# Attention of a decoder layer: the sample's score, key-turn and eviction entries of slots 0 to 4 of twelve, spread between scores, values and turns of the probabilities

## The chip, the cores and the metric

The kernel runs on one core of a Trainium2 chip. The metric is the device time of one execution in microseconds (us). PE is TensorE, ACT is ScalarE, DVE is VectorE, POOL is GpSimd, SP is SyncE, which issues most of the transfers.

## The reference

One layer of a decoder trunk: a half-step feed-forward block, a mixing block with three branches, a second feed-forward block. It serves a prompt of 1024 tokens and eight samples of eight new tokens with 2048 cached keys each. The attention stage of the kernel computes these parts:

```python
def sparse_core(q, k_sel, v_sel, valid):
    s = jnp.einsum("bthd,btkhd->bthk", q, k_sel, preferred_element_type=jnp.float32) * (DH_ATT ** -0.5)
    s = jnp.where(valid[:, :, None, :], s, -jnp.inf)
    p = jax.nn.softmax(s, axis=-1).astype(v_sel.dtype)
    o = jnp.einsum("bthk,btkhd->bthd", p, v_sel)
...
def mem_attend(qm, mk, mv):
    s = jnp.einsum("bthd,bmhd->bthm", qm, mk, preferred_element_type=jnp.float32) * (DH_MEM ** -0.5)
    p = jax.nn.softmax(s, axis=-1).astype(mv.dtype)
    o = jnp.einsum("bthm,bmhd->bthd", p, mv)
```

In `dsa_sample` the keys and values of a sample lie in 16 pages of 128 tokens, found through `page_table`; which keys count is decided before the attention stage and comes into it as a bias (`bias` for the prompt, `bias_s` for the samples).

## The kernel before

The attention stage works off 96 jobs of the prompt, one in each **slot**. A head h (0 to 7) has twelve slots: slots 0 to 7 are the blocks of 128 queries i = 0, 7, 1, 6, 2, 5, 3, 4 of the prompt's own attention, so that slots with few keys, (i + 1) * 128, and many keys alternate; slots 8 to 11 are blocks of the attention to 256 memory tokens. While head h of the prompt is worked off, sample b = h is done beside it, piece by piece. So "head 3" below stands for twelve slots: 12 * 3 + 0 to 12 * 3 + 11, and its sample is number 3.

`attention_plan` writes one list of entries, and every engine walks this list from the first to the last, doing its part of each entry in that order. In a slot s stand, before the change:

- `scores` of job s (PE: three matmuls for each 512 keys, into banks 0/1 or 2/3; DVE: the maximum, then a small product);
- `oturn`, in slot 2 of each head (and slot 10 of odd ones): PE turns finished outputs, 4 blocks at a time;
- `values` of job s - 2 (PE, into bank 6; DVE scales the result: "norm" below);
- `turn` of job s - 1: PE turns the probabilities, up to four blocks of 128 x 128 in one entry;
- `exp` of job s (ACT);
- the sample's entries of this slot, from the table `slots`: `("kt", u)` turns one page u of keys with four transposes, `("sc", g)` makes the sample's scores from four turned pages (PE: eight instructions in bank 5; ACT copies 512 columns out, line L2851).

Each of `turn`, `oturn`, `kt` and some others is a *turning entry*: it needs one of only two banks, `turn_bank = [bank[4], bank[7]]`, and takes them alternately. The entry with an even number is copied out by ACT, the one with an odd number by DVE, and PE may not start a turning entry before the copy of the last but one is finished:

```python
            if turn is not None and turn >= 2:

                wait_turn(pe, turn - 2)
```

Since the number of turning entries before slot 0 differs, the sides change from head to head: of slots 1 to 3 in odd heads (1, 3, 5, 7) page 4 goes to DVE before the change, in even heads to ACT.

The keys' pages come by DMA into `k_ring`, six pages deep. SP issues page n after page n - 6 has been turned, and one page of values (`v_ring`) after each page of keys, 256 KB each. `kt4` holds the turned keys of two groups of four pages, and `sc` of group g waits until its four pages have been copied there.

Of the kernel before, what the change touches and what calls it, by code (L numbers as in the profile page):

```python
# [2331 lines left out]
def attention_plan():  # L2332

    jobs = []
    for h in range(H):  # L2340
        jobs += [("att", i, h) for i in (0, 7, 1, 6, 2, 5, 3, 4)] + [("mem", h % 2 * 4 + i, h // 2) for i in range(4)]
    slots = [
# [6 lines left out]
        [("soft",), ("msc",)],  # L2349
        [("pt", 0), ("pt", 1), ("pt", 2), ("pt", 3), ("pt", 4)],  # L2350
        [("pv",), ("mpt",)],
        [("mpv",), ("ot",)],
        [("mot",)],
        [],
    ]
    plan = []
    turns = 0

    def add(*entry):
        nonlocal turns  # L2360
        turn = None
        if entry[0] in ("turn", "oturn", "kt", "pt", "mpt", "ot", "mot"):
            turn = turns
            turns += 1
        plan.append((entry, turn))

    n = len(jobs)
    add("stack", 0)
    for s in range(n + 3):
        if s < n:  # L2370
            add("scores", s)
        if 0 <= s - 3:

            kind, i, h = jobs[s - 3]
            if kind == "att" and i == 4 and h % 2 == 1:
                add("oturn", s - 3, 0)
                add("oturn", s - 3, 1)
            if kind == "mem" and i % 4 == 3:
                add("oturn", s - 3, 0)
        if 0 <= s - 2 < n:  # L2380
            add("values", s - 2)
        if s >= n - 2:

            add("merge", s - n + 2)
        if 0 <= s - 1 < n:
            kind, i, h = jobs[s - 1]
            blocks = i + 1 if kind == "att" else 2
            for g in range(0, blocks, 4):
                add("turn", s - 1, g, min(4, blocks - g))
        if s < n:  # L2390

            add("exp", s)
            for e in slots[s % 12]:
                add(e[0], s // 12, *e[1:])
            if s % 12 == 8 and s // 12 + 1 < H:
                add("stack", s // 12 + 1)
    return jobs, plan


def attention(nc, sem, mem, bank, bank_t, ident, ident16, qT, kT, qmT, mkT, mv, rq, bias, bias_s, rep, I, O, tail, heads):  # L2400

    jobs, plan = attention_plan()
    at = AT_X + 8192
    def place(name, shape, dt, size):
# [868 lines left out]
```

## Time and profile before

| what | value |
|---|---|
| median of three runs | 3210.53 us (3206.44 to 3211.04) |
| the profiled execution | 3222.86 us, span 3221.3 us |
| PE busy | 3096.3 us of the span, 96% |
| slots 0 to 4 of the eight heads together | 222.10 us, PE busy in 203.70 of them |
| attention stage | from 1684.7 us to about 2157 us of the span |

The page of the profile gives shares of the whole span; the other stages are 85% of it. The attention stage has to be read by itself, slot by slot. A slot begins with the first matmul of its scores (L2684 for the prompt's own attention), so its length is the distance to the first matmul of the next slot's scores.

### The profile page before, as it was taken

The page shows a single profiled execution, that of the slowest core. Times are in us where ns is not written, and L with a number is a line of the kernel's source. Part 1 is how long each engine was busy: PE and PEld are TensorE (multiplying, and loading weights), DVE is VectorE, ACT ScalarE, POOL GpSimd, SP SyncE. Part 2 cuts the span into 40 slices and gives each one's busy share as a digit, 9 for nine tenths or more (in the row PEclk, how much of TensorE's full clock was granted, in tenths as well). Part 3 has the DMA queues.
Part 4 walks back from the last instruction along what each step waited for, and adds up shares of the span by engine and source line. Part 5 has one row for each costly group of instructions (what it writes and reads, how often), then busy time and mean ns, then how long its engine had stood idle before and what let it go on. Part 6 is the DMA issues. An engine that isn't in the chain of part 4 may idle for free. (4 is left out here: it accounts for less than half of the span.)

```text
span 3221.3 us, 51712 instructions
## 1 busy us (share of the span) xinstructions
PE 3096.3 (96%) x19690; PEld 2914.6 (90%) x19690; DVE 1735.3 (54%) x3041; ACT 911.6 (28%) x1616; POOL 668.7 (21%) x415
## 2 busy tenths in 40 slices
PE   7999999999899999999799999889999999999999
PEld 7999999999899999998756666669999999999998
DVE  6333333333669999999535555555645333333333
ACT  5111111111433332334344444441231111111111
POOL 2211221222443321222250000012121212221120
PEclk9999999999999999999888999999999999999999
DMA  3111111111322222221445446344421111111111
GB/s 115 41 45 39 52 39 45 46 46 40 89 82 86 81 85 83 64 74 55 146 133 195 160 146 219 126 164 143 137 73 39 41 46 46 46 39 46 39 46 62
DMA packets 256495, 265.47 MB, mean 82 GB/s; under 512 B 14575, under 2 KB 197458, under 8 KB 256334
## 3 DMA queue, kind: packets, MB, share of 16 engines
q1 hardware_dynamic: 250858, 254.61, 25.0%
q0 software_dynamic: 4128, 4.20, 0.5%
q10 hardware_dynamic: 1348, 4.49, 0.4%
q8 instruction: 103, 1.69, 0.2%
q14 instruction: 58, 0.48, 0.0%
HBM read 226.20 MB, written 37.05 MB: 82 GB/s over the span
## 5 line engine op out<-in xcount | busy, mean ns | idle before, releaser
L331 PE MATMUL bank<-h_hi,w_hi 128*128 128x362 f32 (+1 forms) x3384 | 1119.0, 331 | 25.9 <-DVE sg_ffn L513 7.7
L331 PE MATMUL bank<-h_lo,w_hi 128*128 128x362 f32 (+1 forms) x3384 | 1113.2, 329 | 0.0
L331 PE MATMUL bank<-h_hi,w_lo 128*128 128x362 f32 (+1 forms) x3384 | 1111.9, 329 | 0.0
L331 PEld LDWEIGHTS bank<-h_hi,w_hi 128*128 128x128 f32 x3384 | 638.5, 189 | 33.3 <-issue 18.4
L331 PEld LDWEIGHTS bank<-h_lo,w_hi 128*128 128x128 f32 x3384 | 638.9, 189 | 2.9 <-issue 0.3
L331 PEld LDWEIGHTS bank<-h_hi,w_lo 128*128 128x128 f32 x3384 | 638.7, 189 | 0.0
L388 POOL TENSOR_TENSOR w_lo<-raw,w_hi 128x1024 fp32r<-128x1024 f32 x132 | 316.5, 2406 | 1272.9 <-ACT w_hi L483 1272.9
L550 DVE SCALAR_TENSOR_TENSOR x<-bank,x 128x362 f32<-128x362 f32 (+1 forms) x528 | 280.5, 535 | 213.6 <-PE bank L331 213.6
L331 PE MATMUL bank<-a_hi_ffn,w_hi 128*128 128x362 f32 (+1 forms) x1056 | 347.6, 329 | 5.5 <-DVE x L550 3.8
L331 PE MATMUL bank<-a_lo_ffn,w_hi 128*128 128x362 f32 (+1 forms) x1056 | 346.5, 328 | 0.0
L331 PE MATMUL bank<-a_hi_ffn,w_lo 128*128 128x362 f32 (+1 forms) x1056 | 346.2, 328 | 0.0
L513 DVE TENSOR_TENSOR sg_ffn<-bank,drs_ffn 128x364 f32<-128x364 f32 x132 | 70.4, 535 | 393.9 <-PE bank L331 393.7
L518 DVE TENSOR_TENSOR up_ffn<-bank,drs_ffn 128x364 f32<-128x364 f32 x132 | 70.7, 535 | 372.1 <-PE bank L331 372.1
L483 ACT CAST w_hi<-raw 128x1024 fp32r<-128x1024 f32 x132 | 136.1, 1046 | 426.5 <-PE bank L331 426.5
L1309 POOL TENSOR_TENSOR w_lo<-raw,w_hi 128x1024 fp32r<-128x1024 f32 x53 | 128.3, 2421 | 394.4 <-ACT w_hi L1533 394.4
L331 PEld LDWEIGHTS bank<-a_hi_ffn,w_hi 128*128 128x128 f32 x1056 | 198.4, 188 | 7.9 <-DVE x L550 5.7
L331 PEld LDWEIGHTS bank<-a_lo_ffn,w_hi 128*128 128x128 f32 x1056 | 198.5, 188 | 0.1
L331 PEld LDWEIGHTS bank<-a_hi_ffn,w_lo 128*128 128x128 f32 x1056 | 198.5, 188 | 0.0
L499 ACT CAST a_hi_ffn<-pr_ffn 128x364 fp32r<-128x364 f32 x132 | 65.7, 498 | 433.3 <-DVE pr_ffn L525 433.3
L3048 POOL TENSOR_TENSOR w_lo<-raw,w_hi 128x1024 fp32r<-128x1024 f32 x20 | 50.3, 2520 | 637.0 <-ACT w_hi L3097 637.0
L493 ACT ACTIVATE sg_ffn<-sg_ffn 128x364 f32<-128x364 f32 x132 | 66.9, 509 | 391.3 <-DVE sg_ffn L513 391.2
L1898 DVE MAX8 top<-S 128x8 f32<-128x384 f32 (+5 forms) x192 | 171.2, 891 | 4.1
(370 smaller groups left out, 4138.6 us busy)
## 6 DMA issues: line engine op xcount, KB each, us to landing
raw<-in_w_ffn_in SPq DMA_DIRECT2D x88, 512.0 KB, 3.8
k_ring<-in_cache_k SPq DMA_DIRECT2D x128, 256.0 KB, 4.0
v_ring<-in_cache_v SPq DMA_DIRECT2D x128, 256.0 KB, 4.3
raw<-in_w_in SPq DMA_DIRECT2D x53, 512.0 KB, 4.9
raw<-in_w_ffn_out SPq DMA_DIRECT2D x44, 512.0 KB, 3.4
kept_g<-stage SPq DMA_DIRECT2D x24, 544.0 KB, 3.1
gate<-kept_g SPq DMA_DIRECT2D x24, 544.0 KB, 3.6
x<-x_kept SPq DMA_DIRECT2D x8, 544.0 KB, 4.3
```

The lines of the kernel that those rows point to most:

```text
L331: mm = pe.matmul(out, left, right, start=(start and i == 0 and j == 0), stop=(stop and i == n - 1 and j == 2))
L388: pool.tensor_tensor(self.w_lo[:, u % 3, :], self.raw[:, u % 3, :], self.w_hi[:, u % 3, :].bitcast(F32), ALU.subtract).then_inc(self.low, 1)
L483: act.copy(self.w_hi[:, u % 3, :], self.raw[:, u % 3, :]).then_inc(self.high, 1)
L493: act.activation(self.sg[:, c, 0:w], self.sg[:, c, 0:w], ACT.Silu).then_inc(self.silu_done, 1)
L499: act.copy(self.a_hi[:, t, t0:t0 + w], self.pr[:, c, 0:w]).then_inc(self.prod_high, 1)
L513: dve.tensor_tensor(sg[:, c, 0:w], bank[c][:, 0:w], rs[:, t0:t0 + w], ALU.mult).then_inc(self.scaled, 1)
L518: dve.tensor_tensor(up[:, c % 2, 0:w], bank[3 + c][:, 0:w], rs[:, t0:t0 + w], ALU.mult).then_inc(self.up_scaled, 1)
L550: dve.scalar_tensor_tensor(self.x[:, j, t0:t0 + w], bank[:, 0:w], 0.5, self.x[:, j, t0:t0 + w], ALU.mult, ALU.add).then_inc(self.x_added, 1)
L1309: pool.tensor_tensor(w_lo[:, n % 3, :], raw[:, n % 3, :], w_hi[:, n % 3, :].bitcast(F32), ALU.subtract).then_inc(low, 1)
L1898: after(dve.max(top8[0:rows, :], scores))
L3048: pool.tensor_tensor(w_lo[:, n % 3, :], raw[:, n % 3, :], w_hi[:, n % 3, :].bitcast(F32), ALU.subtract).then_inc(low, 1)
```

## The change

The table of the sample's entries stays as it is, and so does the work. Slots 0 to 4 of each head ("early") place the entries of their slot at three places in place of one: the first entry straight after `scores`, the next two after `values`, and the rest where they all were, after `exp`. Slot 4 has only one entry, `sc 3`, which moves up whole.

```diff
     n = len(jobs)
+    def sample(s, a, b=None):
+
+        if s < n:
+            for e in slots[s % 12][a:b]:
+                add(e[0], s // 12, *e[1:])
+
     add("stack", 0)
     for s in range(n + 3):
+        early = s % 12 < 5
         if s < n:
             add("scores", s)
+            if early:
+                sample(s, 0, 1)
...
         if 0 <= s - 2 < n:
             add("values", s - 2)
+        if early:
+            sample(s, 1, 3)
...
             add("exp", s)
-            for e in slots[s % 12]:
-                add(e[0], s // 12, *e[1:])
+            sample(s, 3 if early else 0)
```

The first place is PE's queue in slots 1 and 2 of an even head (2). `k_high`/`q_stack` with `bias` are the prompt's scores, `bias_s` and `kt` the sample's scores, `mv` and `vp` the values, `pb` the turn of the probabilities, `o_m` the turn of outputs, `k_ring` the turn of pages, four transposes each. Before, from the last matmul of slot 1's scores to the first of slot 3's:

```order
L2686 MATMUL bank<-bias_66,ident_10_58 128x512
L2711 MATMUL bank<-mv_12474,pt_12526 128x128 x2
L2693 MATMUL bank<-ident_55,pb_12525 128x128
L2739 MATMUL bank<-bias_s_67,rep_68 32x512 x4
L2744 MATMUL bank<-kt_121_12518,qbd_12529 32x512 x4
L2724 MATMUL bank<-ident_55,k_ring_12524 128x128 x16
```

```order
L2686 MATMUL bank<-bias_66,ident_10_58 128x256
L2718 MATMUL bank<-ident_55,o_m_12532 128x128 x4
L2707 MATMUL bank<-vp_12520,pt_12526 128x64
L2693 MATMUL bank<-ident_55,pb_12525 128x128 x8
L2739 MATMUL bank<-bias_s_67,rep_68 32x512 x4
L2744 MATMUL bank<-kt_121_12518,qbd_12529 32x512 x4
L2724 MATMUL bank<-ident_55,k_ring_12524 128x128 x16
```

The same two stretches after the change (all line numbers there are higher by ten):

```order
L2696 MATMUL bank<-bias_66,ident_10_58 128x512
L2749 MATMUL bank<-bias_s_67,rep_68 32x512 x4
L2754 MATMUL bank<-kt_121_12518,qbd_12529 32x512 x4
L2721 MATMUL bank<-mv_12474,pt_12526 128x128 x2
L2734 MATMUL bank<-ident_55,k_ring_12524 128x128 x8
L2703 MATMUL bank<-ident_55,pb_12525 128x128
L2734 MATMUL bank<-ident_55,k_ring_12524 128x128 x8
```

```order
L2696 MATMUL bank<-bias_66,ident_10_58 128x256
L2749 MATMUL bank<-bias_s_67,rep_68 32x512 x4
L2754 MATMUL bank<-kt_121_12518,qbd_12529 32x512 x4
L2728 MATMUL bank<-ident_55,o_m_12532 128x128 x4
L2717 MATMUL bank<-vp_12520,pt_12526 128x64
L2734 MATMUL bank<-ident_55,k_ring_12524 128x128 x8
L2703 MATMUL bank<-ident_55,pb_12525 128x128 x8
L2734 MATMUL bank<-ident_55,k_ring_12524 128x128 x8
```

The sample's scores stood between the turns of the probabilities and the four pages; now they stand ahead of all turning entries of the slot, and the turns of the probabilities stand between the second and the third page.

The second place is ACT's queue from slot 1 to the exponentials of slot 2, in the same kind of head. `pt` is the copy of turned probabilities, `kt` of a turned page, `ps` of the sample's scores, `pb` the exponentials. Before:

```order
L2511 COPY pt_12526<-bank 128x128
L2841 ACTIVATE pb_12525,stats_12539<-bank,stats_12539,rq_12475 128x1024
L2851 COPY ps_12527<-bank 128x512
L2532 COPY kt_121_12518<-bank 128x4x128 x2
L2511 COPY pt_12526<-bank 128x512
L2841 ACTIVATE pb_12525,stats_12539<-bank,stats_12539,rq_12475 128x256
```

And after:

```order
L2861 COPY ps_12527<-bank 128x512
L2542 COPY kt_121_12518<-bank 128x4x128
L2521 COPY pt_12526<-bank 128x128
L2851 ACTIVATE pb_12525,stats_12539<-bank,stats_12539,rq_12475 128x1024
L2542 COPY kt_121_12518<-bank 128x4x128
L2861 COPY ps_12527<-bank 128x512
L2542 COPY kt_121_12518<-bank 128x4x128
L2521 COPY pt_12526<-bank 128x512
L2851 ACTIVATE pb_12525,stats_12539<-bank,stats_12539,rq_12475 128x256
```

The copy of the sample's scores and the first of ACT's two pages now stand ahead of the slot's exponentials; the second stays behind them.

## Rows read from the trace of the kernel before

**Rows 1.** The page: span, and PE's busy time, share and instructions.

```profile
span 3221.3 us, 51712 instructions
...
PE 3096.3 (96%) x19690; PEld 2914.6 (90%) x19690; DVE 1735.3 (54%) x3041; ACT 911.6 (28%) x1616; POOL 668.7 (21%) x415
```

**Rows 2.** Page turns in the attention stage: PE's idle time before them, times, by releaser.

```profile
  DVE kt L2532: 17.2, 39
  ACT kt L2532: 17.0, 31
  DMA k_ring<-in_cache_k: 4.7, 6
```

**Rows 3.** Busy time by window: slots 0 to 4 of heads 0 and 4; all eight.

```profile
1684.72:1717.19 32.47, 26.78 (x176) 17.53 (x174) 12.39 (x27) 13.49 (x26) 0.81 (x5) 0.84 0.93 310
...
1923.04:1950.15 27.11, 25.36 (x189) 17.22 (x188) 14.01 (x34) 12.92 (x27) 0.00 (x0) 0.96 0.78 258
...
sum 222.10, PE 203.70 PEld 136.16 DVE 112.41 ACT 103.52 POOL 0.81; mean PE 25.46 PEld 17.02 DVE 14.05 ACT 12.94 POOL 0.10
```

**Rows 4.** Windows, slots 0 to 4 of head 3: length, PE, PEld, DVE, ACT, POOL, clock, DMA.

```profile
1863.66:1867.79 4.13, 3.65 (x28) 2.76 (x27) 2.34 (x7) 2.52 (x7) 0.00 (x0) 1.00 0.01 2
1867.79:1873.65 5.86, 5.51 (x42) 3.30 (x41) 3.47 (x7) 2.55 (x6) 0.00 (x0) 1.00 0.82 291
1873.65:1879.78 6.13, 5.71 (x49) 3.77 (x47) 3.34 (x8) 3.14 (x7) 0.00 (x0) 1.00 0.92 296
1879.78:1886.74 6.96, 6.61 (x56) 4.69 (x54) 3.15 (x7) 2.85 (x6) 0.00 (x0) 1.00 0.93 321
1886.74:1889.92 3.18, 3.18 (x29) 1.79 (x27) 2.21 (x6) 1.73 (x4) 0.00 (x0) 1.00 0.94 317
```

**Rows 5.** Windows, slots 0 to 2 of head 4.

```profile
1923.04:1927.71 4.67, 4.48 (x28) 3.66 (x26) 2.60 (x8) 1.82 (x6) 0.00 (x0) 0.76 0.00 0
1927.71:1933.99 6.28, 5.38 (x42) 3.30 (x41) 3.10 (x7) 3.00 (x6) 0.00 (x0) 1.00 0.88 289
1933.99:1940.00 6.01, 5.60 (x48) 3.79 (x47) 2.98 (x8) 3.34 (x7) 0.00 (x0) 1.00 0.94 316
```

**Rows 6.** The timeline of slots 0 and 1 of head 3.

```profile
1865.26 1.93 PE L2724 MATMUL bank<-ident,k_ring 128*128 128x128 f32 x12
...
1866.76 0.34 SPq L2611 DMA_DIRECT2D k_ring<-in_cache_k  x1
...
1867.23 0.59 ACT L2532 COPY kt<-bank 128x512 f32<-128x512 f32 x1 [0.75 <-PE bank L2724]
...
1867.38 0.66 PE L2724 MATMUL bank<-ident,k_ring 128*128 128x128 f32 x4 [0.19 <-DVE kt L2532]
...
1867.79 0.48 PE L2684 MATMUL bank<-k_high,q_stack 128*128 128x512 f32 x1
...
1868.07 0.69 DVE L2532 COPY kt<-bank 128x512 f32<-128x512 f32 x1 [0.75 <-PE bank L2724]
...
1869.92 0.40 PE L2739 MATMUL bank<-bias_s,rep 64*32 64x512 bf16 x4
...
1870.93 1.21 ACT L2841 ACTIVATE pb<-bank,stats,rq 128x1024 f32<-128x1024 f32 x1 [0.64 <-DVE stats L2897]
...
1871.24 1.09 PE L2724 MATMUL bank<-ident,k_ring 128*128 128x128 f32 x8
...
1872.68 1.22 PE L2724 MATMUL bank<-ident,k_ring 128*128 128x128 f32 x8 [0.35 <-DVE kt L2532]
```

**Rows 7.** Windows of head 0: end of slot 2, slot 3; slot 10, slots 11 to 0.

```profile
1696.60:1702.33 5.73, 2.41 (x20) 1.30 (x13) 1.48 (x3) 1.79 (x5) 0.00 (x0) 1.00 0.96 317
1702.72:1714.01 11.29, 11.29 (x56) 7.75 (x54) 2.73 (x6) 3.22 (x6) 0.00 (x0) 0.55 0.95 334
...
1741.20:1744.40 3.20, 1.75 (x13) 1.14 (x12) 2.83 (x10) 1.03 (x3) 0.00 (x0) 1.00 0.24 87
1744.40:1751.20 6.80, 6.79 (x31) 5.92 (x31) 3.42 (x15) 2.72 (x8) 0.00 (x0) 0.50 0.00 0
```

## The prediction

> **What bounds the kernel now.** I read the page first: PE is busy 96% of a span of 3221.3 us [rows 1], so a change of order can only win where PE waits. Then the windows of the attention stage: slots 0 to 4, the only ones that the change touches, take 222.10 us over the eight heads, and PE is busy in 203.70 of them, so 18.4 us are idle [rows 3]. Head 0 alone has 32.47 - 26.78 = 5.7 of these; the other seven have 12.7, or 1.8 each. Slot by slot, head 3 idles 0.48, 0.35, 0.42 and 0.35 us in slots 0 to 3 and nothing in slot 4 [rows 4]. Head 4 idles 0.9 in slot 1 [rows 5]. Last I asked who ends these waits at the page turns: copies of turned pages by DVE and ACT, 34.2 of 38.9 us (PE's own and the weight loads' idle time added up); pages that had not landed, 4.7 [rows 2]. Neither ACT (12.92 of 27.11) nor DVE (14.01) is full [rows 3]. The bound is PE, with the return of the two turning banks behind it.
>
> **The price of a bank.** All steps below rest on four durations of [rows 6]. Four transposes are issued in 0.41 us (1867.38 to 1867.79), in 0.50 where another group follows at once (my reading of pairs, an estimate between 0.41 and half of 1.09). A copy starts 0.69 after its group (1867.38 to 1868.07) and takes 0.69 on DVE, 0.59 on ACT. So a bank is free again 1.44 us after its group began where DVE copies: the page groups at 1871.24 and 1872.68 show just that. Where ACT copies it is 1.34. The sample's scores cost PE 1.32 (1869.92 to 1871.24) and need no turning bank: they are the cover behind which banks come back.
>
> Before the change, slot 1 is scores, values and a one-block turn (2.13), the sample's scores (1.32), and four pages (1872.68 - 1871.24 = 1.44 for the first pair with its wait, 0.97 for the second): 5.86, as [rows 4] has it. A slot pays one bank wait among its four pages, and the turns of the probabilities pay almost none, since the sample's scores and the prompt's scores stand on either side of them.
>
> **The change part by part.** No instruction is added or taken away; SP's and POOL's queues keep their order. What moves is the place of pages and sample's scores among the others on PE, ACT and DVE, so waits alone change.
>
> *Slots 1 and 3.* The row of turning entries is now page, page, turn, page, page without a gap. The third page needs the bank of the second, or of the turn, whichever is later; the second began 0.50 after the first, so the stretch from the first page to the next slot is 0.50 + 1.44 + 0.85 (the last pair) = 2.79 where DVE has the even places, 2.69 where ACT has. Slot 1: 2.13 less the turn's 0.20, plus 1.32, plus 2.79 = 6.04 in an odd head (before 5.86), 5.94 in an even one (before 6.28 [rows 5]). The even head gains 0.34: there ACT's exponentials of 1.21 us and its copy of the sample's scores stood ahead of the first page's copy, and now stand behind it. Slot 3, the same row behind longer scores and values: +0.2 odd, +0.1 even.
>
> *Slot 2.* The row is seven entries long: turned outputs, page, page, turn, turn, page, page; only values of one block stand in it. The first, third, fifth and seventh share a bank, so the seventh starts three returns after the first: 3 x 1.44 + 0.41 = 4.73 in odd heads, 3 x 1.34 + 0.35 = 4.37 in even ones. Ahead of it, the sample's scores now come straight behind the prompt's, and these are short here (256 keys, about 0.48, an estimate from the 1.9 of slot 1's scores and values). They need the last page of slot 1 copied, 1.34 to 1.44 after it began, of which its own issue and the scores cover 0.83: a new wait of 0.51 to 0.61 on PE, with everything of the slot queued behind it. Slot 2: 0.48 + 0.51 + 1.32 + 4.73 = 7.04 (before 6.13), even 0.48 + 0.61 + 1.32 + 4.37 = 6.78 (before 6.01). This is the largest term, +0.9 and +0.8.
>
> *Slot 4.* The same wait in front of its only entry, behind scores of 384 keys: +0.4 odd, +0.5 even, in a slot of 3.18 that had no idle time [rows 4].
>
> *Slot 0.* Page 0 now starts some 0.3 after the slot began, where PE waited for the turned probabilities of the slot before, and covers that wait. Three pages and the turn follow. Odd heads: 3.65 for 4.13, -0.5. In even heads the clock is low at first (0.76 in the mean [rows 5]); the transposes take twice as long and I find 4.60 for 4.67.
>
> *Pages.* Page 6 is asked for 1.5 us after page 0's turn begins (1865.26, 1866.76 [rows 6]), and the stream runs on at 291 to 321 GB/s with the DMA engines 0.82 to 0.93 busy [rows 4]. Page 0 is turned some 1.3 us earlier, and page 15 later, so the waits for pages (4.7 us in all [rows 2]) should go, except head 0's, whose stream starts when the stage before lets it.
>
> **Sum.** Odd head 3.65 + 6.04 + 7.04 + 7.16 + 3.57 = 27.5, against 26.25 in head 3 [rows 4]. Even head 4.60 + 5.94 + 6.78 + 7.05 + 3.67 = 28.0, against 27.11 in head 4 [rows 3]. Four odd and three even heads make 194.0, plus 1.2 for head 1's slot 0, which runs in the low clock that follows 1744.40 [rows 7]: 195.2 against 222.10 - 32.47 = 189.6. That is +5.6; head 0 is held by its pages up to slot 2 and gets +0.3 in slot 4: **+5.9 us**. The profiled execution (3222.86 us, 1.6 beyond its span) would come to 3228.8; the median of the runs stands 12.3 lower, so 3210.53 + 5.9 = 3216.4. Bounds of the unknown parts: the new waits of slots 2 and 4 lie between 0 (if copies finish under the scores) and 0.6 each, 0 to 9 us over all; slot 2's row between its issue time (3.3) and 4.73. I take the upper ends, since [rows 6] shows the return of 1.44 with no slack, and let the lower ones widen the range.
>
> **Rivals.**
> (a) *Slower still, by the clock.* In head 0 PE is busy in 2.41 of 5.73 us before slot 3, and the clock then falls: slot 3 takes 11.29 for head 3's 6.96. Slot 10 idles 1.45 of 3.20, and 6.80 us at 0.50 follow [rows 7]; heads 2, 4 and 6 idle as long there and keep the clock, so it is near a border. The change shifts those stretches and thins slot 2 (3.3 of issue in 4.7). One fall costs about 1.8 us (head 1's slot 0 alone shows 1.2); three more make 3222. Against it: slot 2 stays two thirds busy. The Trainium skill, "TensorE: Matmul & The Clock Gate", section "A second HAM failure mode: psum-queue depth-cycling", says that PE idling briefly between groups while it cycles through banks lets the clock fall again and again. By that rule every slot 2 would be slow; the trace does not bear it out for four pages in a row, which run at 1.00 [rows 4].
> (b) *Faster, by the pages.* If the page stream set the length of slots 1 to 3, an earlier page 0 would pull all in: 1.3 us in seven heads, 9 us, 3201. For it: 0.93 of the DMA engines. The Trainium skill, "DMA: Bandwidth & Descriptors", section "Specifications", gives about 358 GB/s as the limit of HBM for a core, which the 321 is near. Against it: pages end only 4.7 of 38.9 us. It decides only if PE reaches page 15 before it lands, and my slots 2 and 3 move PE the other way.
> (c) *Faster, as cover.* Spreading hides the bank waits altogether: the seven heads' 12.7 us go, 3198. It needs the turn of the probabilities to find a free bank behind two pages; with two banks and a return of 1.34 it can't.
> (d) *No change.* The waits only change places, and shorter ones than I find in slots 2 and 4 balance slots 0 and 1: 3211.
>
> **How the numbers follow.** The forecast gets 0.48, (a) 0.20, (b) 0.09, (c) 0.06, (d) 0.17. 0.2% is 6.4 us, about what a measurement of this kernel can tell from no change, and the forecast of +5.9 lies just inside it: 0.20 of its 0.48 and all of (a) are slower by more, 0.28 of it and (d) lie within. I give slower 0.40, same 0.45, faster 0.15. The range goes from 3208, below (d), to 3223, above (a); it leaves out (b) and (c).
>
> **What the changed profile would show.** Slot 2 of 6.8 to 7.1 us at full clock, with PE idle about 0.5 ahead of the sample's scores, ended by the copy of a page; slot 4 longer by 0.4 with the same idle time; slot 1 of even heads shorter by 0.3; slot 0 of odd heads shorter by 0.5; no wait for pages outside head 0; slots 5 to 9 unchanged. Wrong would be: slot 2 near 6.1 (the turns do not queue behind pages), or low clock in slots 2 and 3 of any head but 0.

## The result, and the profile after

The changed kernel takes 3224.82 us in the median of ten runs (3217.5 to 3228.67), the kernel before beside it 3214.88 us in ten (3206.44 to 3224.29). The ratio is 1.003, with a 95% interval of 1.002 to 1.0041: slower, by 9.6 us (the two medians differ by 9.9). I had forecast +5.9 us on 3210.53, the median of the first three runs, which was itself 4.3 us under the median of ten. So 3224.82 lies 8.4 us above the 3216.4 that I had forecast, and 1.8 us beyond my range.

The page of the changed kernel, its span and the busy times, against [rows 1]:

```profile
span 3227.1 us, 51680 instructions
...
PE 3100.8 (96%) x19658; PEld 2918.3 (90%) x19690; DVE 1736.7 (54%) x3041; ACT 909.6 (28%) x1616; POOL 668.1 (21%) x415
```

The shares are the same to the digit, so the page can't tell this change. (32 records of matmuls are missing from this trace; the changed kernel's second trace, a2, has 19690 like the kernel before.) The windows can. First slots 0 to 4 of heads 0 and 4 and the sum of the eight heads, then the slots of head 3 one by one, then slots 0 to 3 of head 4, and two stretches at low clock (columns as in [rows 4]):

```profile
1684.95:1712.81 27.86, 23.24 (x174) 14.72 (x174) 12.01 (x26) 12.83 (x25) 0.84 (x5) 1.00 0.92 309
...
1922.01:1949.31 27.30, 25.10 (x188) 16.41 (x188) 13.44 (x33) 12.29 (x26) 0.00 (x0) 1.00 0.84 291
...
sum 223.48, PE 200.91 PEld 132.12 DVE 109.67 ACT 98.22 POOL 0.84; mean PE 25.11 PEld 16.52 DVE 13.71 ACT 12.28 POOL 0.10
...
1860.95:1864.52 3.57, 3.22 (x28) 2.64 (x27) 2.56 (x7) 2.08 (x6) 0.00 (x0) 1.00 0.15 33
1864.52:1870.63 6.11, 5.66 (x42) 3.36 (x41) 3.35 (x7) 2.56 (x6) 0.00 (x0) 1.00 0.86 277
1870.63:1877.74 7.11, 5.87 (x48) 3.80 (x47) 3.55 (x8) 3.81 (x9) 0.00 (x0) 1.00 0.99 343
1877.74:1884.97 7.23, 6.88 (x55) 4.72 (x54) 3.15 (x7) 2.09 (x4) 0.00 (x0) 1.00 0.88 303
1884.97:1888.64 3.67, 3.28 (x29) 1.84 (x28) 1.66 (x6) 1.60 (x4) 0.00 (x0) 1.00 1.05 381
...
1922.01:1925.52 3.51, 3.16 (x28) 2.73 (x26) 2.48 (x8) 2.04 (x6) 0.00 (x0) 0.98 0.13 40
1925.52:1931.52 6.00, 5.65 (x42) 3.36 (x40) 2.95 (x7) 2.66 (x4) 0.00 (x0) 1.00 0.94 308
1931.52:1938.37 6.85, 6.04 (x48) 3.77 (x47) 3.14 (x8) 3.55 (x9) 0.00 (x0) 1.00 0.93 322
1938.37:1945.68 7.31, 6.96 (x54) 4.70 (x54) 3.19 (x7) 2.94 (x8) 0.00 (x0) 1.00 0.92 315
...
1799.30:1806.10 6.80, 6.53 (x31) 5.66 (x30) 3.98 (x14) 2.45 (x7) 0.00 (x0) 0.50 0.00 0
1976.80:1980.20 3.40, 3.40 (x15) 2.91 (x15) 2.01 (x10) 1.59 (x5) 0.00 (x0) 0.50 0.00 0
```

Head 3's slots went from 4.13, 5.86, 6.13, 6.96 and 3.18 us [rows 4] to 3.57, 6.11, 7.11, 7.23 and 3.67. Slot 2 is the large term, and PE idles 1.24 us in it where it idled 0.42. Heads 1 to 7 take 223.48 - 27.86 = 195.6 us for 189.6 before; the forecast was 195.2. The sum of all eight rose by 1.4 only, since head 0's slot 3 had run at low clock before [rows 7] and didn't here.

The two profiled executions differ by 5.8 us (3222.86 and 3228.67), and I had 3228.8 for the second. That match is luck: 0.9 us of it lies between the first slot of the stage and the last slot 4 of head 7, and 4.7 us lies behind that slot, where the change does nothing.

The timeline of PE in head 3, slot 2 and the middle of slot 4 (start, us, line, operands, count, idle time before it and what ended it):

```profile
1870.63 0.36 PE L2694 MATMUL bank<-k_high,q_stack 128*128 128x256 f32 x1
...
1871.68 0.40 PE L2749 MATMUL bank<-bias_s,rep 64*32 64x512 bf16 x4 [0.45 <-ACT kt L2542]
1872.01 1.06 PE L2754 MATMUL bank<-kt,qbd 128*32 128x512 f32 x8
1873.01 0.66 PE L2728 MATMUL bank<-ident,o_m 128*128 128x128 f32 x4
...
1873.67 0.61 PE L2734 MATMUL bank<-ident,k_ring 128*128 128x128 f32 x4
1874.45 0.66 PE L2734 MATMUL bank<-ident,k_ring 128*128 128x128 f32 x4 [0.17 <-DVE qmT L2526]
1874.95 0.66 PE L2703 MATMUL bank<-ident,pb 128*128 128x128 f32 x4
1875.89 0.66 PE L2703 MATMUL bank<-ident,pb 128*128 128x128 f32 x4 [0.28 <-DVE kt L2542]
1876.38 0.60 PE L2734 MATMUL bank<-ident,k_ring 128*128 128x128 f32 x4
1877.33 0.66 PE L2734 MATMUL bank<-ident,k_ring 128*128 128x128 f32 x4 [0.35 <-DVE pt L2521]
...
1886.13 0.40 PE L2749 MATMUL bank<-bias_s,rep 64*32 64x512 bf16 x4 [0.39 <-ACT kt L2542]
```

The groups that share DVE's bank begin at 1873.01, 1874.45, 1875.89 and 1877.33: three returns of 1.44 us, with nothing in between to hide them. The new wait of 0.45 us stands ahead of the sample's scores, and its like of 0.39 in slot 4, each ended by the copy of a page.

What ended the waits ahead of the sample's scores (the first two lines), and ahead of page turns (the last three), in the attention stage (us, times):

```profile
  ACT kt L2542: 3.8, 9
  DVE kt L2542: 2.9, 7
...
  DVE pt L2521: 7.2, 20
  DVE kt L2542: 6.6, 20
  DMA k_ring<-in_cache_k: 2.3, 3
```

The first two lines are sixteen waits of 0.42 us in the mean, one in each slot 2 and each slot 4 of the eight heads. Of [rows 2] the 4.7 us for pages that had not landed have halved, and what remains lies in head 0; the copy of turned probabilities (pt) has come in as the one that pages wait for.

### The profile page after: what moved, and what is told of

It is laid out like the page before. It is cut to its first block and busy times, and to the rows that moved or that the text cites. A ratio compares the mean times of both kernels' runs of the same rounds, so it can differ in the third digit from the quotient of the medians.

```text
span 3227.1 us, 51680 instructions
## 1 busy us (share of the span) xinstructions
PE 3100.8 (96%) x19658; PEld 2918.3 (90%) x19690; DVE 1736.7 (54%) x3041; ACT 909.6 (28%) x1616; POOL 668.1 (21%) x415
## 5 line engine op out<-in xcount | busy, mean ns | idle before, releaser
L331 PEld LDWEIGHTS bank<-h_hi,w_hi 128*128 128x128 f32 x3384 | 638.9, 189 | 33.4 <-issue 18.4
```

The costliest lines, as they stand in the source:

```text
L331: mm = pe.matmul(out, left, right, start=(start and i == 0 and j == 0), stop=(stop and i == n - 1 and j == 2))
```

## The experiments

One number serves all of them. Every run lists its mean granted clock. One straight line for each kernel, all with one common slope, through 232 runs of ten kernels in five sittings gives 1.7 us less for each 0.001 of clock, +-0.1. So besides the ratio, each kernel has a difference to the kernel before *at equal clock*; what stands behind its +- is the standard error. The changed kernel's is +6.6 +-0.6 us. Edits are shown against the changed kernel, where nothing else is said.

**e1: the sample's scores alone, moved up.** Slot 0 and all pages as before.

```diff
-        early = s % 12 < 5
+        early = 0 < s % 12 < 5
...
-        if early:
-            sample(s, 1, 3)
...
-            sample(s, 3 if early else 0)
+            sample(s, 1 if early else 0)
```

> The first entry of slots 1 to 4, the sample's scores, straight after the prompt's scores; all pages stay behind the exponentials, slot 0 as before. Theory (bank return): the sample's scores are lost as cover between the turns of the probabilities and the pages, and they have to wait for the last page of the slot before. Slot 2 about 7.0 us in odd and 6.8 in even heads (before 6.1 and 6.0), slot 4 about 3.6 (before 3.2), slot 1 about 6.3 in odd heads, since ACT's exponentials are no longer behind the sample's scores; slot 0 unchanged. In all +8 to +12 us against before. Rival (the split of the pages is what costs): slots 2 and 4 close to before, at most +2 us.

3230.91 us, ratio 1.0053 (1.0037 to 1.0069), +10.1 +-1.2 at equal clock. The window of head 3's slot 2, and five rows of its PE timeline:

```profile
1865.89:1872.96 7.07, 5.87 (x48) 3.80 (x47) 3.18 (x8) 3.48 (x7) 0.00 (x0) 1.00 0.95 318
...
1866.90 0.40 PE L2747 MATMUL bank<-bias_s,rep 64*32 64x512 bf16 x4 [0.41 <-ACT kt L2540]
...
1868.22 0.66 PE L2726 MATMUL bank<-ident,o_m 128*128 128x128 f32 x4
...
1869.66 0.66 PE L2701 MATMUL bank<-ident,pb 128*128 128x128 f32 x4 [0.17 <-DVE qmT L2524]
...
1871.11 1.09 PE L2732 MATMUL bank<-ident,k_ring 128*128 128x128 f32 x8 [0.28 <-DVE pt L2519]
1872.55 0.66 PE L2732 MATMUL bank<-ident,k_ring 128*128 128x128 f32 x4 [0.35 <-DVE kt L2540]
```

Here the pages stand behind the turns of the probabilities, as before the change, and slot 2 still has 7.07 us, the 0.41 of wait and the same three returns of 1.44. So the loss of slot 2 doesn't come of spreading the pages: it comes of taking the sample's scores, the cover, out of the row of turning entries.

**e2: the pages alone, spread.** Slot 0 as in the changed kernel; in slots 1 to 3 two pages ahead of the turns, the sample's scores behind the exponentials as before, then two pages.

```diff
-            if early:
+            if s % 12 == 0:
                 sample(s, 0, 1)
...
             add("exp", s)
+            if early and s % 12:
+                sample(s, 0, 1)
```

> Slot 0 as in the changed kernel; in slots 1 to 3 the sample's scores stay behind the exponentials and two of the four pages stand ahead of the turns of the probabilities, two behind the sample's scores. Theory (bank return): the sample's scores now cover one of the two waits, so slot 1 is about 5.7 us, slot 2 about 6.0, slot 3 about 6.6, slot 4 3.2, slot 0 3.6: -1.0 to -1.4 us a head, -6 to -10 us in all. Rival (page stream is the bound): pages 11 and 15 are waited for, and the gain stays under 3 us. Rival (splitting the pages is what costs): slots 1 to 3 are longer than before, +3 us or more.

3208.4 us, 0.9989 (0.9979 to 0.9999), -4.7 +-0.8 at equal clock, less than expected; slot 0 alone gives 3.8 of it (e3 below), so spreading the pages of slots 1 to 3 neither gains nor loses clearly. Slots 1 and 2 of head 3, slot 1 of head 4, and for that slot PE's wait and what DVE did before it:

```profile
1861.67:1867.30 5.63, 5.39 (x42) 3.37 (x41) 3.25 (x7) 2.88 (x7) 0.00 (x0) 1.00 0.90 315
1867.30:1873.53 6.23, 5.78 (x49) 3.77 (x47) 3.55 (x8) 3.03 (x7) 0.00 (x0) 1.00 0.92 295
...
1919.02:1925.72 6.70, 5.38 (x41) 3.35 (x40) 2.85 (x7) 3.08 (x6) 0.00 (x0) 1.00 0.87 279
...
1923.30 0.33 PE L2705 MATMUL bank<-ident,pb 128*128 128x128 f32 x1 [1.32 <-DVE kt L2544]
...
1920.69 1.23 DVE L2906 TENSOR_REDUCE stats<-bank 128x1 f32<-128x1024 f32 x1 [1.52 <-PE bank L2698]
...
1922.56 0.68 DVE L2544 COPY kt<-bank 128x512 f32<-128x512 f32 x1
```

With the cover left between the turns and the last two pages, slot 2 keeps 6.23 us. Slot 1 gains 0.2 in odd heads but loses 0.4 in even ones, with PE idle for 1.32 of 6.70. The wait stands ahead of the turn of the probabilities and ends with DVE's copy of page 4. In the old order ACT copies that page in even heads; with the turn behind it, it has fallen to DVE, which does the maximum of the prompt's scores (1.23 us) and the scaling of the outputs first. That I had not foreseen.

**e3: slot 0 alone.** **e4: slot 4 as before, the rest as changed.** These two are one line each:

```diff
-        early = s % 12 < 5
+        early = s % 12 < 1     # e3
+        early = s % 12 < 4     # e4
```

> Only slot 0 is spread. Theory: slot 0 of odd heads 3.6 us for 4.1, of even heads 0.1 to 0.6 less according to the clock, slots 1 to 4 as before, and the waits for pages of slots 2 and 3 (some 2 us outside head 0) gone, since page 0 is turned earlier: -3 to -6 us in all. Rival (page stream sets the length anyway): the waits for pages 11 and 15 grow by what slot 0 gave, 0 +- 2 us.

> The changed kernel with slot 4 as before. Theory: slot 4 falls from 3.63-3.67 us to 3.2 in each head, eight times 0.45: 3.6 us faster than the changed kernel, so +5 to +7 us against before. Rival: the wait moves into slot 5 and nothing is gained, +8 to +10.

e3: 3208.17 us, 0.9986 (0.9974 to 0.9998), -3.8 +-0.9 at equal clock. Slot 0 of heads 3 and 4, and what waits for pages are left (head 0's):

```profile
1846.47:1850.04 3.57, 3.22 (x28) 2.64 (x27) 2.56 (x7) 2.08 (x6) 0.00 (x0) 1.00 0.14 36
1903.80:1907.63 3.83, 3.27 (x29) 2.66 (x27) 2.70 (x11) 2.28 (x6) 0.00 (x0) 1.00 0.24 69
...
  DMA k_ring<-in_cache_k: 3.2, 3
```

No wait for pages is left outside head 0, where the first profile of the kernel before had 1.4 us of them. That doesn't show that slot 0 took them away: the profiles of e1 and e6, both with slot 0 as before, have none there either. Slots 1 to 4 keep their lengths of before. e4: 3220.17 us, 1.0013 (1.0002 to 1.0023), +3.1 +-0.8 at equal clock, which is 3.5 less than the changed kernel, with slot 4 (here head 3's) back at 3.19 us and no idle time:

```profile
1879.91:1883.10 3.19, 3.19 (x30) 1.80 (x28) 2.21 (x6) 2.16 (x6) 0.00 (x0) 1.00 1.05 392
```

**e5: pages first.** Slot 0 as changed; in slots 1 and 3 two pages straight after the prompt's scores, the sample's scores and the other two behind the exponentials; slots 2 and 4 as before. In place of the changed kernel's three `sample` calls stand:

```diff
+            if s % 12 in (1, 3):          # after scores
+                sample(s, 1, 3)
+            if s % 12 == 0:
+                sample(s, 0, 1)
...
+        if s % 12 == 0:                   # after values
+            sample(s, 1, 3)
...
+            if s % 12 in (1, 3):          # after exp
+                sample(s, 0, 1)
+            sample(s, 3 if s % 12 in (0, 1, 3) else 0)
```

> Slot 0 as in the changed kernel, slots 2 and 4 as before, and in slots 1 and 3 two pages straight after the prompt's scores, with values and turns behind them, then exponentials, the sample's scores and two more pages. Theory (bank return): values and the sample's scores each cover one return, so slot 1 is 5.3 to 5.4 us (before 5.86) and slot 3 about 6.4 (before 6.96), with no wait for a bank in them: some 1.5 us a head less than before, -10 to -12 us in all. Rival (page stream): page 15 lands some 20.4 us after page 0 is turned, which is 0.5 us later than PE would reach it; then PE waits for pages 11 or 15 in most heads, slot 3 stays at 6.7 to 7.0, and the gain is -6 to -8 us, little more than that of slot 0 alone.

3208.16 us, 0.998 (0.997 to 0.999), -6.7 +-0.8 at equal clock: as little as the rival of the page stream had said, though not for its reason alone. PE in head 1's slot 2, the waits of page turns for DMA over the stage, and slot 1 of head 4:

```profile
1757.43 0.63 PE L2737 MATMUL bank<-ident,k_ring 128*128 128x128 f32 x4 [1.31 <-DMA k_ring<-in_cache_k]
...
  DMA k_ring<-in_cache_k: 8.6, 11
...
1919.19:1925.38 6.19, 5.39 (x42) 3.36 (x41) 2.77 (x7) 3.17 (x6) 0.00 (x0) 1.00 0.86 275
```

Odd slots 1 shrank to 5.18 us, which PE fills without a wait, and then slot 2 of heads 1 and 3 waited for its last page and took 7.6 and 7.5. Of the 8.6 us, 5.5 lie outside head 0. In even heads slot 1 kept 6.19 us and didn't shrink to the 5.3 to 5.4 of the theory: there PE waits 0.80 us for DVE's copy of a page, behind the same maximum as in e2. So both the page stream and that copy kept the gain down.

**a2 and b2: the changed kernel and the kernel before, once more,** to see which low clock belongs to which.

> The changed kernel once more, for its granted clock in many runs. In the first ten the mean clock was 0.9801 against 0.9816 in 29 runs of the kernel before, and time falls by 1.3 to 2.1 us for each 0.001 of clock. Theory (waits +6, clock +3): ratio 1.002 to 1.004 again, mean clock again 0.001 to 0.002 below that of before, and slots 0 to 4 within 0.1 us of the first profile where the clock is full. Rival (waits alone, the rest is scatter): mean clocks equal within 0.0005 and a difference of 5 to 7 us.

> The kernel before once more, as a measure of scatter: ratio 1.000 with an interval of about 0.1%, mean clock within 0.0005 of that of the runs beside it; a second profile shows which low stretches of the clock recur (slot 10 of odd heads, head 0's slot 3) and which do not. If the low clock of head 0's slot 3 belongs to the wait for page 11, it recurs; if it is chance, it does not.

a2: 3222.35 us, 1.0028 (1.0014 to 1.0042), with the slots of the first profile. b2: 3216.55 us, 1.0003 (0.9992 to 1.0015). Slot 3 of head 0 in it:

```profile
1701.57:1708.53 6.96, 6.72 (x55) 4.67 (x54) 2.67 (x6) 3.18 (x6) 0.00 (x0) 1.00 0.96 297
```

It runs at full clock, 6.96 us for the 11.29 of [rows 7], in the same program: that stretch was chance, and says nothing about the change.

**e6: does a distance between stretches set the clock?** The kernel before, with the score matmuls of slot 5 issued twice (the second time the same values over the first): about 1.06 us more in each head.

```diff
-        for c, k0 in enumerate(range(0, keys, 512)):
+        for c, k0 in [(c, k0) for _ in range(2 if s % 12 == 5 else 1) for c, k0 in enumerate(range(0, keys, 512))]:
```

> The kernel before, with the score matmuls of slot 5 issued twice (the second pass overwrites the first, so nothing else changes): about 1.1 us more of dense PE work in each head, no new wait anywhere. It shifts and lengthens the heads as the changed kernel does, without its waits. Theory A (the clock loss of the changed kernel comes from its new waits in slots 1 to 4): mean clock that of before, time +9 us. Theory B (it comes from the heads' new spacing, which moves the idle stretches of slot 10 of even heads): mean clock 0.001 lower or more, a low stretch in some of heads 2, 4, 6 in the profile, time +11 to +13 us.

3227.03 us in five runs, 1.0033 (1.002 to 1.0046), +9.3 +-1.2 at equal clock for 8.5 of added work, at a mean clock of 0.9808 where the runs beside it had 0.9813. In its profile even heads kept the clock. That is what theory A had said, and nothing supports theory B, though five runs can't exclude a small effect.

**e7 and e9: slot 2 as before, the rest as changed,** in two sittings.

```diff
-        early = s % 12 < 5
+        early = s % 12 in (0, 1, 3, 4)
```

> The changed kernel with slot 2 as before. Theory (slot 2 is the largest term): slot 2 falls from 7.11 and 6.85 us to 6.1 and 6.0, slot 3 keeps 7.2 to 7.3, so 7 to 8 us faster than the changed kernel: 0 to +2 us against before. Rival: the wait for slot 1's last page moves into slot 3's or the turns of slot 2, less than 4 us faster, +5 us against before.

> The changed kernel with slot 2 as before, once more. Theory (slot 2's wait costs clock): mean clock as before, 0.9815 +- 0.0005, about 0.0012 above the changed kernel beside it, ratio 1.000 to 1.0005. Rival (scatter): its mean clock is that of the changed kernel beside it within 0.0004.

e7: 3214.19 us, 1.0000 (0.999 to 1.0009); e9: 3217.42 us, 1.0011 (1.0000 to 1.0021); together +1.4 +-0.6 at equal clock, at a mean clock of 0.9819. Slot 2 of heads 3 and 4 in e7:

```profile
1863.76:1869.99 6.23, 5.82 (x49) 3.77 (x46) 3.54 (x8) 3.46 (x9) 0.00 (x0) 1.00 0.93 294
...
1922.31:1928.66 6.35, 5.73 (x48) 3.79 (x47) 3.06 (x8) 3.67 (x9) 0.00 (x0) 1.00 0.93 316
```

One slot in twelve put back takes away 5.2 of the 6.6 us. I had expected 7 to 8: behind a changed slot 1, slot 2 in the old order takes 6.23 and 6.35 us, a little more than the 6.13 and 6.01 of before.

**a3: the changed kernel, beside e9.**

> The changed kernel a third time, beside the next kernel and the kernel before on one chip, for the granted clock. So far its mean clock is 0.9803 in 19 runs, that of the kernel before 0.9815 in 88; the four kernels with the sample's scores moved up in slot 2 have 0.9803 in 37 runs, all others 0.9815 in 143. Theory (slot 2's wait costs clock): 0.9800 to 0.9806 again, some 0.0012 below before, and a ratio of about 1.003. Rival (scatter between chips and sessions): mean clock within 0.0004 of that of before in the same session, and a ratio of about 1.002, the +6 us that are left at equal clock.

3223.33 us, 1.0028 (1.0016 to 1.0039), at a mean clock of 0.9808 where the kernel before beside it had 0.9820 and e9, with slot 2 put back, 0.9819.

**e8: the place by parity.** What the runs had shown to be best for each kind of slot, put together: slot 0 spread; slot 1 pages first in odd heads, as changed in even ones; slot 3 pages first in even heads, as before in odd ones; slots 2 and 4 as before.

```diff
+            pages_first = s % 12 == 1 and s // 12 % 2 == 1 or s % 12 == 3 and s // 12 % 2 == 0
+            as_changed = s % 12 == 1 and s // 12 % 2 == 0
+            if pages_first:
+                sample(s, 1, 3)
+            if s % 12 == 0 or as_changed:
+                sample(s, 0, 1)
...
+        if s % 12 == 0 or s < n and as_changed:
+            sample(s, 1, 3)
...
+            if pages_first:
+                sample(s, 0, 1)
+            sample(s, 3 if s % 12 == 0 or pages_first or as_changed else 0)
```

> The order that gave each slot its shortest length in the profiles so far: slot 0 spread; slot 1 with two pages first in odd heads (5.18 us) and as in the changed kernel in even ones (6.00); slot 2 as before; slot 3 with two pages first in even heads (6.41), as before in odd ones (6.96); slot 4 as before. Theory: odd heads 3.57 + 5.18 + 6.2 + 6.96 + 3.19 = 25.1, even 3.8 + 6.0 + 6.0 + 6.4 + 3.19 = 25.4, some 1.6 us a head below before: -8 to -12 us. Rival (page stream): odd heads wait for page 11 in slot 2 (up to 1.7 us, as in two heads of the run with two pages first), and the gain stays at that run's -6 us.

3208.18 us, 0.9978 (0.9968 to 0.9988), -9.0 +-0.9 at equal clock: faster than both kernels. Slot 1 of head 3, slots 1 and 3 of head 2, and the waits of page turns for DMA:

```profile
1854.29:1859.47 5.18, 5.18 (x41) 3.35 (x41) 3.26 (x7) 2.88 (x7) 0.00 (x0) 1.00 0.86 289
...
1799.91:1805.91 6.00, 5.65 (x42) 3.36 (x40) 2.94 (x7) 2.66 (x4) 0.00 (x0) 1.00 0.86 283
...
1812.26:1818.67 6.41, 6.41 (x54) 4.69 (x54) 3.12 (x7) 2.98 (x6) 0.00 (x0) 1.00 0.93 292
...
  DMA k_ring<-in_cache_k: 4.5, 5
```

Two of the three have no idle time left. Only one slot of a head is sped up that far, and the waits for pages stay at 4.5 us, where e5 had 8.6; 4.1 of them lie in head 0. In odd heads slots 0 to 2 have the order of e5, yet slot 2 of heads 1 and 3 takes 6.44 and 6.23 us here, for 7.63 and 7.51 there. So those waits for pages are not fixed by a head's own order, and with one profile of each kernel I can't say what sets them. Nor is e8 clearly ahead of e5: 2.3 us at equal clock, +-1.2.

## Why the prediction was right in its mechanism, and which steps failed

*The mechanism held.* The price of a bank, 1.44 us where DVE copies, stands in slot 2 three times in a row, and e1 finds it again in another order. The slots I had worked out as 3.65, 6.04, 7.04, 7.16, 3.57 for odd heads measured 3.57, 6.11, 7.11, 7.23, 3.67 in head 3. For even heads, slots 1 to 3, I had 5.94, 6.78 and 7.05, and head 4 has 6.00, 6.85 and 7.31. Slot 0 of head 4 took 3.51 for my 4.60, because the low clock that I took over from [rows 5] lay further back this time. The signs that I had named came too: all slots 2 of heads 1 to 7 took 6.85 to 7.12 us at full clock, slot 4 grew by 0.4 to 0.5, no wait for pages was left outside head 0, and slot 5 took 4.22 us for 4.24.

*The terms, one by one.* My sum splits into slot 2 (4 x 0.91 + 3 x 0.77 = 5.9), slot 4 (4 x 0.39 + 3 x 0.49 + 0.3 = 3.3), slots 1 and 3 (+0.8), and the rest, slot 0 with the waits for pages (5.9 - 5.9 - 3.3 - 0.8 = -4.1). At equal clock the runs give slot 2 as changed less e7 and e9, 6.6 - 1.4 = 5.2 +-0.7; slot 4 as changed less e4, 3.5 +-0.9; slot 0 as e3, -3.8 +-0.9; and +1.7 remains for slots 1 and 3. The sum of waits is +6.6 for the +5.9 forecast.

Two of these agree partly by luck. Of my -4.1, some 2 us were waits for pages and only 0.1 in all was slot 0 of the three even heads. At full clock that slot goes from 4.29 us (e6, with slot 0 as before) to 3.83 (e3), so slot 0 of seven heads gives 4 x 0.57 + 3 x 0.46 = 3.7 us by itself, and nothing shows what the pages gave. And slot 3 of even heads, where I had +0.1, took 7.31 for 6.96. In the first profile the slots 0 that were too long in my sum and the slots 1 to 3 that were too short in it nearly cancel, which is why 195.6 lies so near to 195.2.

*The steps that failed* are two terms of the sum's last lines, and both made the forecast too low. The larger is the base. "The median of the runs stands 12.3 lower, so 3210.53 + 5.9 = 3216.4" rests on three runs; ten runs beside the changed kernel gave 3214.88, and over all sets the kernel before had medians of 3214 to 3215.5. That is 4.3 of the 8.4 us that I was off. The other is the clock, which the sum puts at nothing; I had kept it apart, as rival (a) with a chance of 0.20. Over three sets the changed kernel's mean clock is 0.9805 (31 runs, standard error 0.00025), the kernel before's 0.9816 (111 runs, 0.00015); 0.0011 at 1.7 us for each 0.001 is 1.9 us. The waits, 6.6 for 5.9, add 0.7, and the rest is scatter of the median. 6.6 + 1.9 = 8.5 us of difference stands beside 9.6, 9.0 and 9.0 us from the three ratios. So (a) was right in sign, with 1.9 us where I had allowed three falls of 1.8. No row gave that 1.8; the slope does now: 6.8 us at half clock take 0.0011 off the mean clock of 3220 us, and so cost 1.8 us (an estimate). By that estimate the clock's part is the price of about one more such stretch in each execution.

The range failed by the same base. Its upper end, 3223, had 6.6 us above the forecast for the clock, and the base used up 4.3 of them. On the base of ten runs the same sum gives 3220.8 and the same range ends at 3227.4, above the 3224.82 measured.

*Where* the clock is lost stays open. Rival (a) looked for it in slot 2, but in the five profiles with the sample's scores moved up there (changed three times, e1, e4) I found low clock in it once, 3.4 us in head 0 of a3. The profiles of e2, e5 and e9, where slot 2 has the scores where they were, have 3.4 to 5.4 us of it in the same place. Low stretches begin where they did before, in slots 10 and 11 and at the end of the stage, the changed kernel's first profile at 1799.30 and 1976.80, and again at 2154.30; but these come and go in the same program as well. The three kernels whose slot 2 has the scores moved up (changed, e1, e4) have 0.9804 in 49 runs, the others 0.9816 in 183, and slot 2 put back has 0.9819. That is a link across kernels and no cause: e8, with slot 2 as before, had 0.9806 in its nine runs. The Trainium skill, "TensorE: Matmul & The Clock Gate", section "A second HAM failure mode: psum-queue depth-cycling", would have the clock fall where PE idles between groups as it cycles through banks. No trace here shows that in slot 2, with its four waits in 7.11 us; the lower mean clock is the most that could be said for it.

*The other rivals.* (b), faster by the pages: wrong for this change, since in e3 page 0 is turned earlier and slots 1 to 4 keep their lengths. The stream it spoke of can bind: e5 waited 5.5 us for pages outside head 0. (c), faster as cover: wrong; sixteen new waits came in, and PE's idle time in slots 0 to 4 rose from 18.4 to 223.48 - 200.91 = 22.6 us. (d), no change: wrong at equal clock by 6.6 +-0.6 us.

## What to carry to other kernels

Where two buffers go round between an engine and its copies, work that needs neither of them is the cover. Before moving it, count the entries that are left in a row and multiply by the full return time: here 1.32 us of cover, moved by a few places, cost 0.9 us in one slot of twelve, and the same spreading of the pages of slots 1 to 3 with the cover left in its place cost nothing clear (e2 at -4.7 beside e3 at -3.8). What gained was slot 0, where a page filled a wait that PE had anyway. What a copying engine has ahead of the copy decides as much as the order on the engine that waits, so the best place can differ with parity: page 4 behind DVE's maximum of 1.23 us cost slot 1 of even heads 0.4 us in e2. For changes of 0.3%, take the base from ten runs or more, and compare at equal clock.

## What the runs showed of the hardware that was not expected

The mean granted clock of a run explains about half of the variance between runs of one program: 1.7 us for each 0.001, with 2.7 us of scatter left where 3.8 were before. Within one program the low stretches come and go: head 0's slot 3 took 11.29 us at 0.55 once and 6.96 at 1.00 the next time, with the same instructions.

The windows show 343 GB/s in slot 2 and 381 in slot 4 of the changed kernel, in stretches of 7.11 and 3.67 us. The Trainium skill, "DMA: Bandwidth & Descriptors", section "Specifications", gives about 358 GB/s as the limit of HBM for a core, as its half of what two cores share. The row of slot 4 lies above that, with one core at work. It is a short row, though: the same trace has the DMA engines 1.05 busy in it, more than they can be, because a window counts each packet whole where it starts. Slots 1 to 4 of head 3 together, 24.12 us, show 320 GB/s. So the row of slot 4 is no evidence against the page's figure.
